# Input projections of a mixer packed into fewer matmul passes, its vector work reordered, its scaled residual rows moved to GpSimd

## The reference, cut to what matters

```python
proj = h @ w_in[l]                       # 1024 -> 1888 columns
a_in, b_q, b_k, b_v, c_in, d_cq, d_ckv, d_kr = split(proj)   # 512, 256, 128, 128, 512, 192, 128, 32
a   = depthwise_conv(a_in[:256] * sigmoid(a_in[256:]), ...)  # 31 taps
o_a = silu(layer_norm(a))
o_b = attention(rope(rms_norm(b_q)), rope(rms_norm(b_k)), b_v)
u, sv = split(gelu(c_in));  o_c = u * (sgu_w @ layer_norm(sv) + sgu_b)
o_d = attention(rms_norm(d_cq) @ w_uq, rms_norm(d_ckv) @ w_ukv, d_kr)      # latent attention
h   = layer_norm(ALPHA * h + concat(o_a, o_b, o_c, o_d) @ w_out[l])
```

## Time and profile before

| | us |
|---|---|
| median of 3 runs | 1802.2 (1802.15 to 1802.97) |
| the profiled execution, its own time | 1802.04 |
| its span, first to last instruction | 1800.2 |
| mean granted TensorE clock | 0.999 |
| VectorE, ScalarE, POOL busy | 1322.4, 962.1, 98.8 |
| mixer 0, from its first projection to the start of its last output unit | 59.13 to 157.82 |
| mixer 1, the same stretch | 362.57 to 461.49 |

### The profile page before, as it was taken

One profiled execution on the slowest core, in us unless ns is written; L12 is line 12 of the kernel. 1 busy time (PEld: TensorE's weight loads), 2 busy tenths in 40 slices (PEclk: granted clock), 3 DMA queues, 4 the chain that ended last, 5 costly groups with the idle time before them and its releaser, 6 DMA issues.

```text
span 1800.2 us, 29127 instructions
## 1 busy us (share of the span) xinstructions
PE 1769.4 (98%) x10801; PEld 1556.3 (86%) x10801; DVE 1322.4 (73%) x1774; ACT 962.1 (53%) x1293; POOL 98.8 (5%) x90
## 2 busy tenths in 40 slices
PE   6999999999999999999999999999999999999999
PEld 6977989897889988888998988888888887888887
DVE  6898877898987787666887656666666677557666
ACT  5566555456655545444655555444544468655443
POOL 1000200000200000000170000000000000000000
PEclk9999999999999999999999999999999999999999
DMA  9625756553576537565534734555555541525553
GB/s 326 189 97 172 257 182 210 163 151 103 178 248 210 186 125 257 187 198 173 165 112 152 255 120 165 194 192 187 185 188 188 200 148 48 188 94 190 188 197 126
DMA packets 232387, 319.06 MB, mean 177 GB/s; under 512 B 12150, under 2 KB 202518, under 8 KB 231798
## 3 DMA queue, kind: packets, MB, share of 16 engines
q1 hardware_dynamic: 226598, 295.97, 49.4%
q0 software_dynamic: 5424, 20.35, 3.5%
q10 hardware_dynamic: 288, 1.69, 0.2%
HBM read 313.79 MB, written 4.19 MB: 177 GB/s over the span
## 4 chain that ended last, share of the span: by engine, by line
PE 90%; DVE 5%; ACT 3%; issue 2%; DMA 0%; DVEq 0%; ACTq 0%
PE bank L1033 20%; PE bank L1018 20%; PE bank L735 17%; PE bank L1036 10%; PE bank L911 7%; PE bank L744 3%; PE bank L758 2%; DVE w_lo L2349 1%; PE bank L763 1%; PE bank L796 1%; ACT w_hi L1691 1%; PE bank L1115 1%; DVE x L2346 1%; DVE work L2346 1%; PE bank L1235 0%
## 5 line engine op out<-in xcount | busy, mean ns | idle before, releaser
L2349 DVE TENSOR_TENSOR w_lo<-raw,w_hi 128x2048 fp32r<-128x2048 f32 (+1 forms) x283 | 644.7, 2283 | 201.0 <-ACT w_hi L1691 198.9
L1691 ACT ACTIVATE w_hi<-raw 128x2048 fp32r<-128x2048 f32 (+1 forms) x278 | 528.3, 1903 | 286.3 <-PE bank L1033 159.0
L1033 PE MATMUL bank<-xt_both,w_hi 128*128 128x512 f32 x1600 | 400.3, 392 | 0.0
L735 PE MATMUL bank<-xt_both,w_hi 128*128 128x256 f32 (+1 forms) x1904 | 346.7, 284 | 0.2
L1033 PEld LDWEIGHTS bank<-xt_both,w_hi 128*128 128x128 f32 x1600 | 291.6, 189 | 54.6
L735 PEld LDWEIGHTS bank<-xt_both,w_hi 128*128 128x128 f32 (+1 forms) x1904 | 295.2, 190 | 2.5 <-issue 1.5
L1691 ACT ACTIVATE work<-bank 128x256 f32<-128x256 f32 (+3 forms) x288 | 120.2, 428 | 283.5 <-PE bank L1036 257.0
L735 PE MATMUL bank<-xt_both,w_lo 128*128 128x256 f32 (+1 forms) x952 | 269.2, 283 | 0.0
L1036 PEld LDWEIGHTS bank<-xt_both,w_lo 128*128 128x128 f32 x1600 | 218.3, 190 | 15.6
L1036 PE MATMUL bank<-xt_both,w_lo 128*128 128x256 f32 x1600 | 223.1, 282 | 0.0
L1018 PE MATMUL bank<-w_hi,act_hi 128*128 128x512 f32 x528 | 206.7, 392 | 0.2
(11 more groups left out here) (352 smaller groups left out, 1979.7 us busy)
## 6 DMA issues: line engine op xcount, KB each, us to landing
raw<-in_ffn_wi SPq DMA_DIRECT2D x88, 1024.0 KB, 5.1
raw<-in_ffn_w_up SPq DMA_DIRECT2D x44, 1024.0 KB, 5.1
raw<-in_ffn_wo SPq DMA_DIRECT2D x44, 1024.0 KB, 4.8
raw<-in_ffn_w_down SPq DMA_DIRECT2D x22, 1024.0 KB, 5.3
raw<-in_w_in SPq DMA_DIRECT2D x14, 1024.0 KB, 5.7
raw<-in_ssd_in_proj SPq DMA_DIRECT2D x14, 1024.0 KB, 5.3
raw<-in_w_out SPq DMA_DIRECT2D x8, 1024.0 KB, 4.8
raw<-in_even_out_proj SPq DMA_DIRECT2D x8, 1024.0 KB, 4.9
```

The costliest lines, as they stand in the source:

```text
L735: ins = first(mm(dst, w[s][:, k, c0:c0 + m], xt[v][:, k, :], start=k == 0 and p == 0, stop=k == KT - 1 and p == 2))
L1033: first(mm(bank[b][:, :], w[0][:, k, P * j:P * j + P], xt_both[:, k, :, :].rearrange("p v t -> p (v t)"), start=k == 0, stop=False))
L1691: return act.activation(dst, src, ACT.Copy)
L2349: return dve.tensor_tensor(out=out, in0=in0, in1=in1, op=op)
```

## The change

- The columns are packed anew. Unit 3 is now keys and latent keys/values, both feature-major. Unit 6 is the 192 latent query columns and the 32 of `d_kr` (224 columns). Values (128 columns) and `sv` (256 columns) are one token-major product of 384 columns; its weights come as two units, 5 with feature tiles 0 to 4 and 7 with tiles 5 to 7. `IN_ORDER` becomes 0, 1, 2, 3, 6, 4, 5, 7. Units 3, 5, 6 and 7 are loaded by two DMAs each; a split is as wide as its unit.
- TensorE: unit 4 moves ahead of `norm_ready`; the packed product stands around `scores(0)` as `values_tokens(0)` and `values_tokens(1)`, into banks 2 and 3. `qss` is in bank 4.
- ScalarE: the copies and squares follow the new banks; gelu and value copy come once per token tile; the split of the first output unit stands ahead of `exponentials(0)`.
- VectorE: `gain_rows` and `bias_rows` are gone. One turn of taps fewer stands ahead of `value_norm` and one more behind `gate_c`; the splits and `value_stats` move as shown below.
- POOL: `scale_rows`, the same four instructions as in `apply_wide`, right behind the `sgu_b` loads.

```diff
-IN_ORDER = (0, 1, 2, 3, 6, 7, 4, 5)
+IN_ORDER = (0, 1, 2, 3, 6, 4, 5, 7)
+IN_DMAS = (1, 1, 1, 2, 1, 2, 2, 2)
+IN_COLUMNS = {3: ((768, 128), (1728, 128)), 6: ((1536, 192), (1856, 32)), 5: ((896, 128), (1280, 256)),
+              7: ((896, 128), (1280, 256))}
+IN_TILES = {5: (0, 5), 7: (5, 3)}
+IN_SIZE = {6: KT * 224, 5: 5 * 384, 7: 3 * 384}
...
 # TensorE, mixer(l)
-                w = weights(f"in{l}.3", (KT, 256))
-                claim(3, f"{t}.kv")
-                first = First()
-                feature_major(bank[3][:, 0:T], w, 0, P, first)
-                for tt in range(TT):
-                    ins = token_major(bank[3][:, T + P * tt:T + P * tt + P], w, tt, P, P, first)
-                ins.then_inc(bank_full[3], 1)
-
-                pair_fm(f"in{l}.6", 2, f"{t}.cq")
+                pair_fm(f"in{l}.3", 3, f"{t}.kv")
+
+                w = weights(f"in{l}.6", (KT, 224))
+                claim(2, f"{t}.cq")
+                first = First()
+                feature_major(bank[2][:, 0:T], w, 0, P, first)
+                feature_major(bank[2][0:96, T:2 * T], w, P, 96, first).then_inc(bank_full[2], 1)
...
-                w = weights(f"in{l}.7", (KT, 160))
-                claim(3, f"{t}.ckv")
-                first = First()
-                feature_major(bank[3][:, 0:T], w, 0, P, first)
-                ins = feature_major(bank[3][0:96, T:2 * T], w, 64, 96, first)
-                ins.then_inc(bank_full[3], 1)
+                ins.then_inc(bank_full[4], 1)
+
+                pair_fm(f"in{l}.4", 6, f"{t}.u")
 
                 pe.wait_ge(norm_ready, seen.next(norm_ready))
...
-                pair_fm(f"in{l}.4", 6, f"{t}.u")
+                early, late, passed = weights(f"in{l}.5", (5, 384)), weights(f"in{l}.7", (3, 384)), First()
+                def values_tokens(tt):
+                    claim(2 + tt, f"{t}.vs{tt}")
+                    dst, tokens = bank[2 + tt][:, 0:384], slice(P * tt, P * tt + P)
+                    for k in range(KT):
+                        w, kk = (early, k) if k < 5 else (late, k - 5)
+                        for p, (s, v) in enumerate(PASSES):
+                            ins = mm(dst, xt[s][:, k, tokens], w[v][:, kk, :], start=k == 0 and p == 0,
+                                     stop=k == KT - 1 and p == 2)
...
+                values_tokens(0)
                 pe.wait_ge(rot_ready, seen.next(rot_ready))
                 scores(0)
-                pair_tm(f"in{l}.5", 7, f"{t}.sv")
+                values_tokens(1)
 # VectorE, mixer(l)
-                dve.wait_ge(wide_in, 32 * (1 + 2 * l))
-                gain_rows(0)
                 taken(f"{t}.ag")
...
-                more_taps(11, 3)
-                split()
+                more_taps(11, 2)
                 dve.wait_ge(mem_out, START_SAVED + 32 * l)
...
                 split()
-                more_taps(17, 1)
+                split()
+                more_taps(15, 1)
...
-                step(bias_rows(0))
-                gain_rows(1)
                 invert_a()
                 low_half(3)
-                bias_rows(1).then_inc(x_done, 1)
 # POOL, mixer(l), behind the sgu_b loads
+                scale_rows()
```

More of the change, by code:

```diff
@@ L198, in weight_units @@
     for l in range(2):
-        units += [(f"in{l}.{j}", 1) for j in IN_ORDER] + [(f"mla{l}", 9)]
+        units += [(f"in{l}.{j}", IN_DMAS[j]) for j in IN_ORDER] + [(f"mla{l}", 9)]
         units += [(f"out{l}.{j}", 1) for j in OUT_ORDER]
@@ L637, in split_waits @@
             begun = place[split_order[q - RING]][0] + 2 if q >= RING else None
-            return slot, value, begun, KT * {"ssd10": 16, "in0.7": 160, "in1.7": 160}.get(split_order[q], 256)
+            name = split_order[q]
+            if name.startswith("in"):
+                return slot, value, begun, IN_SIZE.get(int(name[-1]), UNIT)
+            return slot, value, begun, KT * {"ssd10": 16}.get(name, 256)
         block = ctx.enter_context(nc.Block())
@@ L1998, in mixer @@
                 drained(f"{t}.cq", act.activation(m_sq[0:64, 1, :], b[0:64, T:2 * T], ACT.Square))
+                taken(f"{t}.kv")
+                act.activation(m_sq[:, 2, :], m_c[:, 2, :], ACT.Square).then_inc(sq_ready, 1)
                 split()
[L2000 to L2003, removed]
                 b = full(f"{t}.cms")
@@ L2047, in mixer @@
                 exponentials(0)
-                split()
-                b = full(f"{t}.sv")
-                drained(f"{t}.sv", act.activation(c_s[:, :, :], b[:, :], ACT.Gelu_apprx_tanh))
                 b = full(f"{t}.u")
                 drained(f"{t}.u", act.activation(c_u[:, :, :], b[:, :], ACT.Gelu_apprx_tanh))
+                for tt in range(TT):
+                    b = full(f"{t}.vs{tt}")
+                    copy(g_v[:, tt, :], b[:, 0:P])
+                    drained(f"{t}.vs{tt}", act.activation(c_s[:, tt, :], b[:, P:3 * P], ACT.Gelu_apprx_tanh))
                 b = full(f"{t}.sw")
@@ L2786, in mixer @@
                 t = f"m{l}"
-                def gain_rows(tt):
-                    step(tt_(x[:, tt, :], z[:, tt, :], wide[:, 0, :], ALU.mult))
-                def bias_rows(tt):
-                    return tt_(x[:, tt, :], x[:, tt, :], wide[:, 1, :], ALU.add)
                 split()
                 split()
-                dve.wait_ge(wide_in, 32 * (1 + 2 * l))
-                gain_rows(0)
                 taken(f"{t}.ag")
@@ L2883, in value_stats @@
                 def value_stats():
-                    taken(f"{t}.sv")
+                    for tt in range(TT):
+                        taken(f"{t}.vs{tt}")
                     for tt in range(TT):
@@ L2947, in operand @@
                     split_operand(u % 2, mix[:, k:k + 2, :])
+                maxima(0)
+                more_taps(17, 1)
+                finish(0)
                 more_taps(19, 1)
-                maxima(0)
+                maxima(1)
+                value_stats()
                 more_taps(21, 1)
-                finish(0)
-                split()
-                value_stats()
-                maxima(1)
-                more_taps(23, 1)
                 latent_rope()
@@ L2959, in mixer @@
                 low_half(0)
-                more_taps(25, 1)
+                split()
+                more_taps(23, 1)
                 value_norm()
@@ L2965, in mixer @@
                 low_half(1)
+                more_taps(25, 1)
                 finish(2)
@@ L3316, in apply_wide, with scale_rows @@
             def apply_wide(next_load, z_count, behind):
-                pool.wait_ge(wide_in, seen.next(wide_in, 0))
                 pool.wait_ge(z_ready, seen.next(z_ready, z_count))
                 pool.wait_ge(unit_split, place[behind][3] + 1)
+                scale_rows()
+                pool.wait_ge(x_done, seen.next(x_done))
+                pool.sem_inc(wide_used, 1)
+                load_wide(*next_load)
+            def scale_rows():
+                pool.wait_ge(wide_in, seen.next(wide_in, 0))
                 for tt in range(TT):
@@ L3534, in mixer @@
                 for j in IN_ORDER:
-                    columns(f"in{l}.{j}", w, *((1728, 160) if j == 7 else (256 * j, 256)))
+                    if j not in IN_COLUMNS:
+                        columns(f"in{l}.{j}", w, 256 * j, 256)
+                        continue
+                    s, k = turn_for(f"in{l}.{j}"), place[f"in{l}.{j}"][1]
+                    k0, nk = IN_TILES.get(j, (0, KT))
+                    n, at = sum(n for _, n in IN_COLUMNS[j]), 0
+                    for c0, m in IN_COLUMNS[j]:
+                        sp.dma_start(raw[:, k, 0:nk * n].rearrange("p (k n) -> p k n", k=nk)[:, :, at:at + m],
+                                     w.rearrange("(k p) n -> p k n", p=P)[:, k0:k0 + nk, c0:c0 + m]).then_inc(s, 16)
+                        at += m
                 name = f"mla{l}"
```

21 lines of the change are left out of this document (11 added, 10 removed).

## The result

The changed kernel takes 1810.7 us (median of 5 runs, 1809.7 to 1811.0), against 1802.15 for the kernel before in the same session: ratio 1.0046, 95% interval 1.0035 to 1.0057. The forecast was 1809.4, in a range from 1799.8 to 1812.8. The profiled execution has a span of 1809.1 us in place of 1800.2, at a mean granted clock of 0.996.

What follows compares the result with a forecast made beforehand. Both engines were taken as full, with VectorE's lateness at the value norm, where TensorE's `branch_c` waits, deciding. 1802.04 + 4.18 (mixer 0) + 3.16 (mixer 1) = 1809.4 us; range 1799.8 to 1812.8.

Steps and rivals of the forecast that it cites:

- POOL's rows: Early taps of each mixer: POOL's four row instructions block VectorE's taps in turns, +9.36 us a mixer.
- VectorE's waits: Ahead of the value norm: waits for a rounded weight and a bank vanish, -1.06 us in mixer 0; -3.3 in mixer 1.
- The gain row, the tap turn and the splits: VectorE work removed ahead of mixer 0's value norm: -1.22, -1.68 and -0.57 us.
- Behind the meeting: From `branch_c`, which needs VectorE's value norm, to the last output unit: slack and two TensorE waits absorb 0.65 us of lateness.
- TensorE ahead: TensorE's work before `branch_c`: repacked products save 5.72 us a mixer, with the packed product taken at 8.44.
- TensorE's idle time up to the rotations: Ahead of the rotations TensorE waits some 6.5 us, for unit 4's split and `norm_ready`.
- the freely passing taps: Rival: taps beside POOL don't block, so the mixers gain about 8.2 us, 1793.8 us; chance 0.15.
- The partly hidden hold: Rival: one or two POOL instructions a mixer hide in other VectorE work or waits, 1804.7 or 1800.0 us; chance 0.15.
- The clock: Rival: after idling at `norm_ready` TensorE runs at half rate, 0 to 1.7 us more a mixer, up to 1812.8; chance 0.08.
- The turning point: Block of VectorE's taps by POOL below which the changed kernel is faster: about 5.7 us a mixer.

Runs made afterwards that it cites:

- the version without rows: The change with the mixers' scaled residual rows made by neither POOL nor VectorE, so the output differs from the kernel's; 1796.0 us.
- the version with memsets: The change with each of POOL's four row instructions per mixer replaced by a memset of the same 128x1024 tile; 1795.0 us, ratio 0.9964.

## Why the prediction was right, and where it wasn't

The mechanism held: the change makes VectorE late at the value norm, by POOL's rows, and the packing itself costs nothing. Its terms for mixer 0, from the first gate (72.8 in both) to the end of the value norm, measured 61.97 us against 56.39:

- **POOL's rows: +9.36 forecast, +8.64 measured** in mixer 0, 8.32 in mixer 1. Not 4.68 but 4.3 a pair; right in kind, 8% too high. The held taps, between each two POOL rows one, were as described.
- **VectorE's waits: -1.06 forecast, +0.31 measured** (0.43 + 1.17 + 0.84 + 0.22 now; 0.44 + 0.85 + 0.34 + 0.72 before). This is the one term that was wrong in kind. I struck the waits for engines "that would now be ahead of VectorE", and had shown in the next part that TensorE would idle behind VectorE there. A TensorE that starts the rotations late, and at half clock, delivers the scores late: the 1.17 us. In mixer 1 I struck 3.3; by the rows with idle time its waits were 5.64 and are 5.33. The bank waits went as forecast (1.26 and 0.88 became 0.49 and 0.23), but the largest are now 1.97 for gate a, of which 1.10 is the gain row that left the gap, and 1.08 for the rounding of unit 6. The chain of waits shows the transfer of that unit with 7.10 us ahead of the rounding; a version with the loads moved wasn't tried.
- The gain row, the tap turn and the splits (-1.22 - 1.68 - 0.57) stand. With the measured hold and waits they give +5.48; the trace has +5.58. In mixer 1 the same sum is +4.54; `branch_c` starts there at 442.65 in place of 432.95, 9.70 later, of which mixer 0 brought 5.09: +4.61.
- **Behind the meeting: -0.65 forecast**, -0.45 measured (5.54 late at `branch_c` and 5.09 at the last output unit).
- **TensorE ahead: -5.72 forecast.** The packed matmuls have a median of 334 ns in the view by line, and 24 of them take 4.39 us, 0.183 each, so the product costs 8.76 and not 8.44: -5.40. It decided nothing.
- **TensorE's idle time up to the rotations: 6.5 forecast**, 1.05 for the split of unit 4 and 5.01 for `norm_ready`, together 6.06, measured. Of the two figures in the prediction, 6.5 is for both waits, and "some 5" is for the one ahead of the rotations.

The two errors, -0.7 and +1.4 in mixer 0, partly cancel: +4.2 forecast, +5.1 measured. In mixer 1 they are -1.0 and +3.0, against the gain row's -1.22, which I had left at nothing: +3.2 forecast, +4.2 measured. That the total came within 1.3 us of the trace is in part luck: the terms missed by up to 3.0 us and partly made up for each other.

Of the rivals, the freely passing taps are refuted by the 11.99. The partly hidden hold is refuted too: even the 4.1 us instruction of mixer 1 is a turn, not a saving, and VectorE's waits of 1.97 and 1.08 fell outside. The clock was not a rival but a part of the result: it fell, as the earlier trace rows had it, and by the traces cost about 2 us here and 4.4 in the kernel before with POOL's rows (5.0 by the times). The turning point, 5.7 us of hold a mixer, is nearer to 4: without a hold the kernel gains 6 us and not 8.2. In the version without rows VectorE's list of mixer 0 is shorter by 3.43 us (3.47 forecast, without the waits): new waits of 0.42 and 0.46 us (a rounded weight, ScalarE) at 80 and 92 us make up for the ones that went. The rest was lost behind the meeting. There the prediction added 0.65 to the gain, which it had found for a VectorE that is late; measured are 0.45 where the clock stays (28.10 in place of 28.55 us from `branch_c` to the last output unit) and a loss of 0.83 in mixer 0 of that version, where the clock fell (29.38). In the version with memsets it stays in both mixers, and by its trace they gain 7.7 us.

## What to carry to other kernels

An idle POOL is no free helper for a busy VectorE: one that reads SBUF takes turns with it, instruction by instruction, and here gave VectorE 8.6 us of standing still in exchange for the 4.9 us that the rows cost it (four of 1.22). Look at where VectorE meets TensorE before handing work over. One row early in the stage and three in idle time ahead of the end cost nothing that can be measured (1795.7, against 1796.0 without rows), but a row put in front of TensorE's last operand made it wait 1.3 us more in each mixer. A wait struck from a sum must be checked against who has become late. Where a new idle time of TensorE of several us appears, add the half clock behind it, and a few matmuls of zeros in the gap are a cheap test of its size; read that size from the trace, since here it was as small as the spread of the runs.

## What the hardware did that I had not expected

- POOL's `tensor_tensor` holds a `tensor_scalar` with a single tensor input as fully as a tap: 9.69 us for four that take 1.14.
- Moved to where VectorE's list is thin, the same 10 us of POOL cost 5 us more (1815.9 and 1816.0, against 1810.7), with a hold of the same size (8.45 and 8.55 against 8.64). TensorE idled 7.3 to 7.5 us in one piece and ran at half clock behind it. How much of the 5 us that explains was not isolated: neither version was run with zeros in the gap.
- The clock fell after as little as 2.1 to 2.4 us of waiting at `branch_c` in some places (2.03 us of work in mixer 0 of the version with the rows on VectorE, and of the one without rows, after 2.42 and 2.12) and not in others (1.15 in mixer 1 of the first, after 2.11, and in both mixers of the change, after 2.12). Where it fell, the way to the last output unit took 29.4 to 29.6 us in place of 28.1. What tells the places apart was not tried.
